# Second product of a wide unit's logits as two products over 64 partitions each, in different halves of the array and different banks

## What is computed

```python
z = (jnp.einsum('bhqd,bhkd->bhqk', q, k).astype(jnp.float32) * (HEAD_DIM ** -0.5)
     + bias.astype(jnp.float32)[None, :, None, None])
causal = k_pos[None, :] < q_pos[:, None]
log_beta = jax.nn.log_sigmoid(z)
log_stay = jnp.where(causal, log_beta - z, 0.0)
log_after = lax.cumsum(log_stay, axis=3, reverse=True) - log_stay
w = jnp.where(causal, jnp.exp(log_beta + log_after), 0.0)
return jnp.einsum('bhqk,bhkd->bhqd', w.astype(v.dtype), v)
```

## Time and profile before

| | |
|---|---|
| median of 3 runs | 1657.03 us (1656.65 to 1657.3) |
| profiled execution | 1656.68 us |
| its span, first to last instruction | 1654.7 us |
| mean granted TensorE clock | 0.999 |
| TensorE busy | 1644.6 us (99%), 9956 products |
| VectorE, ScalarE, GpSimd busy | 694.0, 516.9, 569.2 us |
| DMA | 157.55 MB, mean 95 GB/s |

### The profile page before, as it was taken

The page is one execution under the profiler, slowest core; times in us unless marked ns, Lnnn a source line. Parts: engine busy times, 40 slices in busy tenths (PEclk is TensorE's granted clock), DMA queues, the critical chain, the costliest instruction groups (busy, mean ns, idle before and its releaser), DMA issues.

```text
span 1654.7 us, 24985 instructions
## 1 busy us (share of the span) xinstructions
PE 1644.6 (99%) x9956; PEld 1520.6 (92%) x9956; DVE 694.0 (42%) x1156; ACT 516.9 (31%) x1001; POOL 569.2 (34%) x402
## 2 busy tenths in 40 slices
PE   9999999999999999999999999999999999999998
PEld 8999999999988889999889998899888998899987
DVE  7785868859421222466334330032211331022333
ACT  7565655656322222422245220022100220012111
POOL 5212212112212111232884334733347324652510
PEclk9999999999999999999999999999999999999999
DMA  5202112021276677442552111321113111221211
GB/s 161 66 26 68 39 39 73 21 63 42 96 241 196 208 230 228 164 143 91 172 178 77 52 52 64 102 65 50 53 64 115 49 42 64 89 83 46 89 51 57
DMA packets 145006, 157.55 MB, mean 95 GB/s; under 512 B 9119, under 2 KB 99899, under 8 KB 144892
## 3 DMA queue, kind: packets, MB, share of 16 engines
q1 hardware_dynamic: 144746, 155.93, 29.7%
q10 hardware_dynamic: 146, 0.04, 0.0%
HBM read 136.96 MB, written 18.98 MB: 94 GB/s over the span
## 4 chain that ended last, share of the span: by engine, by line
PE 89%; DVE 6%; ACT 3%; issue 1%; POOL 0%; DVEq 0%; ACTq 0%; POOLq 0%
PE ps L1126 51%; PE ps L1418 10%; PE ps L1423 10%; PE ps L1421 9%; DVE sp L1901 2%; PE ps L1320 2%; DVE zc L1893 1%; PE ps L1276 1%; PE ps L1286 1%; PE ps L1364 1%; PE ps L1332 1%; ACT sp L1604 1%; PE ps L1303 1%; PE ps L1302 1%; DVE br L1849 1%
## 5 line engine op out<-in xcount | busy, mean ns | idle before, releaser
L1126 PE MATMUL ps<-xh,wh 128*128 128x364 f32 (+1 forms) x956 | 323.7, 339 | 0.7 <-DVE xl L1874 0.6
L1126 PE MATMUL ps<-xh,wl 128*128 128x364 f32 (+1 forms) x956 | 313.8, 328 | 0.0
L1126 PE MATMUL ps<-xl,wh 128*128 128x364 f32 (+1 forms) x956 | 313.8, 328 | 0.0
L1113 POOL TENSOR_TENSOR wl<-raw,wh 128x1024 fp32r<-128x1024 f32 x106 | 256.3, 2418 | 19.1 <-POOL wh L1110 18.9
L1126 PE MATMUL ps<-yh,wh 128*128 128x384 f32 (+1 forms) x768 | 250.5, 326 | 0.2 <-DVE yl L2070 0.2
L1126 PE MATMUL ps<-yh,wl 128*128 128x384 f32 (+1 forms) x768 | 250.5, 326 | 0.0
L1110 POOL CAST wh<-raw 128x1024 fp32r<-128x1024 f32 x106 | 111.1, 1048 | 404.8 <-issue 383.1
L1126 PE MATMUL ps<-yl,wh 128*128 128x384 f32 (+1 forms) x768 | 250.3, 326 | 0.0
L1728 ACT ACTIVATE ts<-tt 128x384 f32<-128x384 f32 (+1 forms) x96 | 48.8, 508 | 553.8 <-DVE tt L2082 553.7
L1027 POOL CAST wh<-raw 128x1024 fp32r<-128x1024 f32 x48 | 50.8, 1059 | 479.1 <-issue 205.3
L1126 PEld LDWEIGHTS ps<-xh,wh 128*128 128x128 f32 x956 | 179.7, 188 | 17.0 <-issue 15.3
(11 more groups left out here) (190 smaller groups left out, 2632.2 us busy)
## 6 DMA issues: line engine op xcount, KB each, us to landing
raw<-in_w_down SPq DMA_DIRECT2D x112, 256.0 KB, 2.9
raw<-in_w_in SPq DMA_DIRECT2D x80, 256.0 KB, 3.5
cache<-in_cache_k SPq DMA_DIRECT2D x64, 256.0 KB, 3.6
cache<-in_cache_v SPq DMA_DIRECT2D x64, 256.0 KB, 3.7
raw<-in_w_up SPq DMA_DIRECT2D x64, 256.0 KB, 3.2
raw<-in_w_out SPq DMA_DIRECT2D x48, 256.0 KB, 2.9
gates<-gst SPq DMA_DIRECT2D x16, 544.0 KB, 6.0
gb<-gates SPq DMA_DIRECT2D x16, 544.0 KB, 5.7
```

The lines of the kernel that those rows point to most:

```text
L1113: g.tensor_tensor(low[:, :], raw[n % 3][:, :], f32(high[:, :]), ALU.subtract).then_inc(w_split, 1)
L1126: ins = mm(out, lhs[:, k * P:(k + 1) * P], rhs[:, x], start=(first and a == 0 and m == 0), stop=(last and a == n - 1 and m == 2))
```

## The change

In the logits step the products of qd stay, for both banks. The second product is no longer qz by kx over 128 rows. For columns 0 to 511 it takes the own 64 rows of qz and kx. For the columns from 512 on (wide units only) it takes the other 64 rows: there qz no longer holds zeros but, in columns 512 to 1023, the low parts of those queries again, and in columns 0 to 511 the high parts of keys 512 to 1023 (wide units have queries from 512 on only, so both fit in one tile). The two products of a wide unit lie in different halves of the array's rows and write different banks. The copies are made in the evacuations: VectorE subtracts the query columns from 512 on into the other rows too, ScalarE copies the key columns from 512 on too. A second semaphore, z_upper, tells of the second product of a wide unit. The clearing of qz and its semaphore go.

```diff
@@ logits, TensorE @@
                     if i == 0 and u == 0:
                         pe.wait_ge(cols_made, 2)
-                        pe.wait_ge(qz_zero, 2)
                     for a in range(0, width(u), 512):
                         z = min(width(u), a + 512)
-                        for m, x in enumerate((qd[h], qz[h])):
-                            ins = mm(ps[:, ZB * 512 + a:ZB * 512 + z], x[:, t * P:(t + 1) * P], kx[h][:, a:z],
-                                     start=(m == 0), stop=(m == 1))
-                    ins.then_inc(z_full, 1)
+                        mm(ps[:, ZB * 512 + a:ZB * 512 + z], qd[h][:, t * P:(t + 1) * P], kx[h][:, a:z], start=True, stop=False)
+
+                    r, o = own(h), other(h)
+                    z = min(width(u), 512)
+                    mm(ps[:, ZB * 512:ZB * 512 + z], qz[h][r, t * P:(t + 1) * P], kx[h][r, 0:z], start=False, stop=True).then_inc(z_full, 1)
+                    if width(u) > 512:
+                        z = width(u) - 512
+                        mm(ps[:, (ZB + 1) * 512:(ZB + 1) * 512 + z], qz[h][o, t * P:(t + 1) * P], qz[h][o, 0:z],
+                           start=False, stop=True).then_inc(z_upper, 1)
@@ evacuation of Q and K, ScalarE @@
                     if k == Q and i:
                         act.wait_ge(z_full, i * UNITS)
+                        act.wait_ge(z_upper, i * WIDE_UNITS)
...
                         if k == K:
+                            x, y = max(a, 512), min(z, SEQ)
+                            if x < y:
+                                A(qz[h][other(h), x - 512:y - 512], src[r, x - a:y - a], ACT.Copy)
                             ins = A(kx[h][r, a:z], src[r], ACT.Copy)
@@ start, VectorE @@
-            for h in range(2):
-                V_.memset(f32(qz[h])[HD - h * HD:2 * HD - h * HD, :], 0.0).then_inc(qz_zero, 1)
@@ evacuation of Q, VectorE @@
                     for h in range(2):
                         r = slice(h * HD, h * HD + HD)
+                        x = max(a, 512)
+                        if x < e:
+                            V_.scalar_tensor_tensor(out=qz[h][other(h), x:e], in0=src[r, x - a:e - a], scalar=HD ** -0.5,
+                                                    in1=f32(qd[h][r, x:e]), op0=ALU.mult, op1=ALU.subtract)
                         ins = V_.scalar_tensor_tensor(out=qz[h][r, a:e], in0=src[r, 0:e - a], scalar=HD ** -0.5, in1=f32(qd[h][r, a:e]),
                                                       op0=ALU.mult, op1=ALU.subtract)
@@ cap, VectorE @@
                     v.wait_ge(z_full, i * UNITS + u + 1)
+                    if width(u) > 512:
+                        v.wait_ge(z_upper, i * WIDE_UNITS + u + 1)
```

More of the change, by code:

```diff
@@ L281, in hybrid_layer @@
         th_made, tl_made = sem("th_made"), sem("tl_made")
-        z_full = sem("z_full")
+        z_full, z_upper = sem("z_full"), sem("z_upper")
         zc_ready = sem("zc_ready")
@@ L292, in hybrid_layer @@
         tap_made = sem("tap_made")
-        conv_out, conv_in, qz_zero = sem("conv_out"), sem("conv_in"), sem("qz_zero")
+        conv_out, conv_in = sem("conv_out"), sem("conv_in")
         ends_made, ends_turned, end_rows_made, ends_out = (sem(n) for n in ("ends_made", "ends_turned", "end_rows_made", "ends_out"))
@@ L335, in width, with own, other @@
             return (UNIT[u][1] + 1) * P
+        WIDE_UNITS = sum(width(u) > 512 for u in range(UNITS))
+        assert all(width(u) > 512 for u in range(WIDE_UNITS))
+        def own(h):
+            return slice(h * HD, h * HD + HD)
+        def other(h):
+            return own(1 - h)
         def groups(u):
```

## The result

The changed kernel takes 1672.68 us (median of 4 runs, 1671.74 to 1672.91) where the kernel before takes 1657.16 (4 runs): ratio 1.0093, 95% interval 1.0075 to 1.011. It is slower by 15.5 us; 11 had been forecast, with a range, 1661 to 1674, that holds the result near its upper end. The profiled execution took 1671.74 us, its span is 1670.0, so 15.3 us lie inside the span.

The account below looks back on a forecast made before the run. TensorE, busy 99% of the span, was taken to bound the kernel. 9.6 us for four pairs + 1.6 at the start = +11.2 on 1656.7, 1667.9; with the median 0.35 above, 1668; range 1661 to 1674.

Parts of the forecast that it names:

- The sign and the mechanism: Whole kernel: slower (0.87); in the logits, row halves overlap, but all 64 second products pay for changing the array's partition.
- So changing the partition of the array and back costs 0.28 us: TensorE, each 64-row visit between full-array products: 0.09 lost going in, 0.19 coming out, read from transposes in the trace.
- the bound of 0.34: Upper bound for one 64-row visit on TensorE, in us, with all of the 0.05 for a second weight load.
- The eight transposes of the earlier trace: Eight transposes over 64 rows between dense products, at 33.07 to 34.24 us, from which the 0.28 us was read.
- a second weight load ... in two units a pair: Inside a visit, may add 0.05 us, showing only where the second half is as long as the first.
- The sum for a pair: TensorE, per head pair: 16 x 0.28 = 4.5, + 2 x 0.05, - 1.18 for overlap: 3.4 us more.
- The waits: TensorE waits at logits and value products, 1.2 us a pair: 1.0 is filled, leaving 2.4 us a pair, 9.6 for four.
- The copies: Extra query and key copies on VectorE and ScalarE: 0.77 + 0.84, together 1.6 us, once at the start; later pairs nothing.
- rival A: Logits: partition change costs 0.28, but halves run one after the other, 4.7 us more than the forecast: 1673; chance 0.14.
- B: Rival: products like these pay nothing for the partition change; 1656.7, no change, at best 1652.3; chance 0.10 together with D.
- C: Rival: only coming out of a visit costs (0.19), the first half's weights being loaded ahead; 1662.5; chance 0.12.
- D: Rival: array stays whole for 64 partitions, no half overlaps, only the start counts; 1658.6; chance 0.10 together with B.

## Why the prediction was right, point by point

- The sign and the mechanism: right. The halves overlap (run with both in one half, 4.4 us for 4.7), each of the 64 visits pays, the narrow ones for nothing (9.0 us of the 15.5).
- "So changing the partition of the array and back costs 0.28 us": this term was too small; it is 0.39, and that is above even the bound of 0.34 that I had set for it. The eight transposes of the earlier trace rows show all four parts. I took two of them at the borders (0.09 and 0.19) and set the 0.05 inside aside as "a second weight load ... in two units a pair". I now read it as the third part, the long first product behind the change, which every visit has. With eight short transposes it showed as 0.05 only; with one long product it is 0.105. Why it is less there no run shows.
- The sum for a pair: 16 x 0.395 = 6.3, less the 1.18 of the overlap. A second correction goes the other way. Behind a product of 128 columns the dense products of the kernel before already took 0.11 us more than their columns (a step of 0.11 behind it for 0.06, then 0.22 for 0.165), and a visit swallows that: four units a pair, 0.44. That makes 4.7 us a pair on TensorE, where I had 3.4.
- The waits: I let 1.0 of 1.2 us be filled. All of them were: 4.7 - 1.2 = 3.5, the measured lengthening of a pair. That term was 0.2 too low, in the other direction.
- The copies: at the start 1.6 forecast, 1.8 by the two waits, in the changed kernel and with the copies alone (0.77 as said for the token block; 1.0 for the keys where I had 0.84). The runs with the copies alone are 2.0 longer. Later pairs covered the copies, as said.
- Some luck is in the number. With 0.39 in place of 0.28 and the other terms as they were, the forecast would have been some 7 us higher, above the range; the products of 128 columns took back 1.8 of that. And the range reached up to 1674 for the sake of rival A, which is wrong, not for a dearer visit.
- Rival A gave 1673, nearly the measured time, and is wrong: its mechanism, halves one after the other, is what the run with both in one half shows, at 1677. A time that fits doesn't make a rival true; the two starts at 155.69 told it from the forecast.
- B fell with the steps (0.4 us a visit), C with the exit and the entrance both being there, D with the two halves starting together.

The rows of the correction for 128 columns, unit 5 of the second pair in the kernel before (timeline of PE):

```profile
176.36 0.27 PE L1276 MATMUL ps<-kx,qz 128*128 128x128 f32 x1
176.47 0.38 PE L1126 MATMUL ps<-xh,wh 128*128 128x360 f32 x1
176.69 0.33 PE L1126 MATMUL ps<-xl,wh 128*128 128x360 f32 x1
```

## What to carry to other kernels

Where TensorE is what the kernel waits for, price the visit before a product is cut to 64 rows for the sake of overlap: 0.39 us here for going in and out of the partition, to be set against the columns that the overlap frees. By my estimate it pays only when more than some 850 columns (0.39 us at 0.235 for 512) run beside others in one visit, and products with no partner should keep the whole array; over 96 rows nothing was paid. When a price is read from a trace, count everything between two undisturbed steps, the inside of the visit too, and choose sample rows whose instructions are as long as the new one.

## What the runs showed that I had not expected

- The first product behind a change of partition is 0.105 us longer than the next of its kind, on both sides of the change (0.49 and 0.39 us in the records of the run with both products in one half), and its weights are not loaded ahead.
- A product in plain 4-byte type is two instructions of two cycles a column each (2 x 0.43 us for 512 columns at a granted clock of 0.999 of 2.4 GHz), where a transpose of such data is one (0.109 us for 128 columns), and an fp32r product is one of some 1.1 cycles (0.235 us for 512).
- The recorded start of a product behind transposes comes 0.08 us early, and its own step is that much longer, so single steps there mislead; the sum over both does not.
